# Two attention stages of a two-block network: the first unit's scores later in TensorE's order, no matrix steps behind its turning

## The reference, cut to what matters

```python
def softmax_attend(q, k, v, scale):
    s = jnp.einsum('bqhd,bkhd->bhqk', q, k).astype(jnp.float32) * scale
    p = jax.nn.softmax(s, axis=-1).astype(v.dtype)
    return jnp.einsum('bhqk,bkhv->bqhv', p, v)

def diff_attend(q, k, v, lam, scale):
    s = jnp.einsum('bqhmd,bkhmd->bhmqk', q, k).astype(jnp.float32) * scale
    p = jax.nn.softmax(s, axis=-1)
    a = (p[:, :, 0] - lam * p[:, :, 1]).astype(v.dtype)
    return jnp.einsum('bhqk,bkhv->bqhv', a, v)

y = (jax.nn.sigmoid(g_na) * ((o_na * jax.nn.silu(z_na)) @ w_br_l[0])
     + jax.nn.sigmoid(g_mla) * ((o_mla * jax.nn.silu(z_mla)) @ w_br_l[1])
     + jax.nn.sigmoid(g_diff) * ((o_diff * jax.nn.silu(z_diff)) @ w_br_l[2]))
return y @ w_out_l
```

## Time and profile before

| | us |
|---|---|
| median of 3 runs | 2687.6 |
| lowest and highest | 2682.66, 2688.82 |
| the profiled execution, its own time | 2682.66 |
| its span | 2680.9 |
| TensorE busy in the span | 2482.4 (93%) |
| VectorE busy | 1368.1 (51%) |
| ScalarE busy | 1189.5 (44%) |
| GpSimd busy | 639.4 (24%) |

### The profile page before, as it was taken

How to read it: one execution, slowest core, us unless ns; L and a number is a source line. 1 busy time by engine, 2 the same in 40 slices (tenths; PEclk the granted TensorE clock), 3 DMA queues, 4 the chain that set the end, 5 groups by cost and what they waited for, 6 DMA issues and landing times. The chain is left out here.

```text
span 2680.9 us, 34890 instructions
## 1 busy us (share of the span) xinstructions
PE 2482.4 (93%) x13664; PEld 1960.9 (73%) x13664; DVE 1368.1 (51%) x2120; ACT 1189.5 (44%) x2002; POOL 639.4 (24%) x392
## 2 busy tenths in 40 slices
PE   5997879999998998899997999999999979989988
PEld 3784447888888887568996767577767858768778
DVE  2206667433445766437665534542566444454665
ACT  1824324522327433344654345564366234565362
POOL 1437640000006434110001442003301116403310
PEclk8998988999999999998998999999999999999999
DMA  6326842433324332655664231222222323334333
GB/s 228 86 80 213 290 162 71 118 95 95 102 79 122 107 88 70 219 174 142 190 186 128 63 93 46 59 64 76 71 63 66 92 63 95 107 91 116 89 100 111
DMA packets 416682, 302.11 MB, mean 113 GB/s; under 512 B 10306, under 2 KB 388776, under 8 KB 416520
## 3 DMA queue, kind: packets, MB, share of 16 engines
q1 hardware_dynamic: 415408, 299.45, 38.0%
q10 hardware_dynamic: 1112, 0.44, 0.1%
HBM read 298.80 MB, written 1.05 MB: 112 GB/s over the span
## 5 line engine op out<-in xcount | busy, mean ns | idle before, releaser
L207 POOL TENSOR_TENSOR weights_lo<-wslots,weights_hi 128x1024 fp32r<-128x1024 f32 x158 | 386.4, 2455 | 867.5 <-ACT weights_hi L197 620.5
L197 ACT ACTIVATE weights_hi<-wslots 128x1024 fp32r<-128x1024 f32 x398 | 418.1, 1054 | 288.1 <-PE psum L260 233.0
L260 PE MATMUL psum<-input_hi,weights_hi 128*128 128x512 f32 (+1 forms) x1400 | 501.2, 358 | 4.5 <-PEq L2696 1.8
L260 PE MATMUL psum<-input_hi,weights_lo 128*128 128x512 f32 (+1 forms) x1400 | 488.4, 349 | 0.0
L260 PE MATMUL psum<-input_lo,weights_hi 128*128 128x512 f32 (+1 forms) x1400 | 488.2, 349 | 0.0
L207 DVE TENSOR_TENSOR weights_lo<-wslots,weights_hi 128x1024 fp32r<-128x1024 f32 x240 | 298.7, 1253 | 193.6 <-ACT weights_hi L197 193.3
L260 PEld LDWEIGHTS psum<-input_hi,weights_hi 128*128 128x128 f32 x1400 | 265.1, 189 | 44.4 <-issue 7.5
L260 PEld LDWEIGHTS psum<-input_lo,weights_hi 128*128 128x128 f32 x1400 | 263.8, 188 | 38.3 <-issue 3.4
L260 PEld LDWEIGHTS psum<-input_hi,weights_lo 128*128 128x128 f32 x1400 | 263.9, 189 | 37.7
L260 PE MATMUL psum<-ffn_hidden_hi,weights_hi 128*128 128x512 f32 (+1 forms) x512 | 172.8, 338 | 0.0
L260 PE MATMUL psum<-ffn_hidden_hi,weights_lo 128*128 128x512 f32 (+1 forms) x512 | 172.5, 337 | 0.0
(11 more groups left out here) (439 smaller groups left out, 4857.0 us busy)
## 6 DMA issues: line engine op xcount, KB each, us to landing
wslots<-w_in SPq DMA_DIRECT2D x132, 512.0 KB, 4.0
wslots<-ffn_w SPq DMA_DIRECT2D x128, 512.0 KB, 4.2
wslots<-ada_w SPq DMA_DIRECT2D x96, 512.0 KB, 4.9
wslots<-ssd_w_in SPq DMA_DIRECT2D x49, 512.0 KB, 4.0
wslots<-w_ada SPq DMA_DIRECT2D x48, 512.0 KB, 4.5
wslots<-gla_w_in SPq DMA_DIRECT2D x25, 512.0 KB, 3.8
wslots<-w_br SPq DMA_DIRECT2D x24, 512.0 KB, 3.6
wslots<-ssd_w_out SPq DMA_DIRECT2D x16, 512.0 KB, 4.9
```

The lines of the kernel that those rows point to most:

```text
L197: act.activation(self.part(self.whi_r, n), self.slot(n), ACT.Copy)\
L207: engine.tensor_tensor(self.part(self.wlo_r, n), self.slot(n), self.part(self.whi, n), ALU.subtract)\
L260: ins = pe.matmul(out_of(self.bank(g)), l, r, start=first and i == 0, stop=last and i == len(pairs) - 1, skip_group_check=not (first and l ...
```

## The change

TensorE's order at the start of both functions: `scores(0)` moves behind some of the steps, and all steps up to the first mark now stand ahead of `scores(1)`; none is left behind `turn(0)`. VectorE does `normalise(0)` or `combine(0)` ahead of `vector_second`. In the last unit of `attend_maps`, `middle` lies at a quarter of the unit's steps.

```diff
--- before.py
+++ after.py
@@ -2779,18 +2779,17 @@
                     for _ in range(a, e):
                         next(products)
 
-                lead = marks[0] if near else S // 2
+                lead = 0 if near else S
+                steps(0, lead)
                 scores(0)
-                steps(0, lead)
+                steps(lead, marks[0])
                 for n in range(N):
                     if n + 1 < N:
                         scores(n + 1)
-                    if n == 0:
-                        steps(lead, max(S, lead))
                     turn(n)
                     if n:
                         values(n - 1)
-                    steps(start(n) if n else max(S, lead), marks[n])
+                        steps(start(n), marks[n])
                 values(N - 1)
                 for _ in products:
                     pass
@@ -2867,8 +2866,8 @@
 
                 fill.vector_first(dve)
                 maxima(0)
+                normalise(0)
                 fill.vector_second(dve)
-                normalise(0)
                 for n in range(N):
                     b.split_weights(dve, "dve", fill.lead(start(n)))
                     if n + 1 < N:
@@ -3138,7 +3137,7 @@
         return marks[n - 1] if n else 0
 
     def middle(n):
-        return (start(n) + marks[n]) // 2 if n == N - 1 else marks[n]
+        return (3 * start(n) + marks[n]) // 4 if n == N - 1 else marks[n]
 
     st = ExitStack()
     with st:
@@ -3202,20 +3201,20 @@
                         next(products)
 
                 lead = S // 2
+                steps(0, lead)
                 scores(0)
-                steps(0, lead)
+                steps(lead, marks[0])
                 for n in range(N):
                     gq, h = units[n]
                     if n + 1 < N:
                         scores(n + 1)
-                    if n == 0:
-                        steps(lead, S)
                     turn(n)
                     if n:
                         values(n - 1)
                     if gq and h == 2:
                         turn_rows(gq - 1)
-                    steps(start(n) if n else S, middle(n))
+                    if n:
+                        steps(start(n), middle(n))
                 values(N - 1)
                 for _ in products:
                     pass
@@ -3307,8 +3306,8 @@
 
                 fill.vector_first(dve)
                 maxima(0)
+                combine(0)
                 fill.vector_second(dve)
-                combine(0)
                 for n in range(N):
                     gq, h = units[n]
                     b.split_weights(dve, "dve", fill.lead(start(n)))
```

## The result

The changed kernel is slower: 2710.5 us (median of 4, 2706.4 to 2710.8) against 2685.3 for the kernel before (2682.7 to 2688.8); ratio 1.0102, interval 1.0078 to 1.0128. The ratio takes in all 15 executions of the changed kernel on record (2700.8 to 2720.2, median 2715.0), so it says 27 us where the two medians say 25. The forecast was 2720.2, slower with a chance of 0.94. The profiled execution of the changed kernel took 2715.9 us, 33 more than the profiled one of before.

What follows compares the result with a forecast made beforehand. TensorE's own order of work was taken as the bound. Waits 24.5 us, less 0.3, plus 8.4 for the clock gave 32.6 on 2682.66, so 2715.3; the runs' median lies 4.9 higher, forecast 2720.2, range 2705 to 2734.

Steps and rivals of the forecast that it cites:

- What bounds the kernel: Four stages, pairs with r = 1 and maps in both layers: TensorE's own order of work is the clock.
- Rival C: Late starts absorbed where another engine sets a stage's end; 2700 us if half were absorbed; chance 0.07.
- The stages with r = 0: attend_pairs with r = 0, both layers: the list of steps stays the same, cost 0.
- The waits: New TensorE waits at the four stages' openings: 6.2, 5.8, 6.8 and 5.7, in all 24.5 us.
- the sum: Count of TensorE's waits in each opening, from the stage's issue up to unit 1's steps; 24.5 us over four stages.
- rival B: Clock falls more than once per stage, unit 2 in layer 1's pairs loses 1 us; centre 2730 us, chance 0.15.
- VectorE's swap: Openings: branch split now follows unit 0's normalising, ahead of unit 1's maxima; 2.28 us in layer 0, 1.22 in layer 1.
- The clock: Half-clock work behind the waits in the four stages: 2.1 us each, 8.4 in all, bounds 0 and 22.
- Rival A: Waits without a slower clock, layer 1's being broken by short work: 2711.8 us, chance 0.17.
- Rival E: No change: both effects of Rival D at a smaller size; chance 0.03.
- Rival D: Faster: clock rises sooner at each opening, unit 1's exponentials ready when turn(0) ends; 2680.5 us, chance 0.03.
- The last unit: End of the maps: steps moved by middle are hidden, VectorE's gating product behind subnorm gives -0.3 us in layer 1.

Runs made afterwards that it cites:

- e7: Against the kernel before, the change in attend_pairs alone, attend_maps left as before: ratio 1.0080.
- e6: The changed kernel with identity products put on TensorE in the places where it waits: ratio 1.0115 against the kernel before.
- e4: The changed kernel with the last S/2 steps ahead of the first mark put behind scores(1): ratio 1.0087 against the kernel before.
- e5: The changed kernel with VectorE's maxima of unit 1 ahead of branch and weight splits, layer 0 only: ratio 1.0117 against the kernel before.
- e11: The changed kernel with unit 1's maxima and normalising or combining ahead of VectorE's splits, layer 0 only: ratio 1.0088 against the kernel before.
- e1: The changed kernel again, no edit, in more rounds: 2711.5 us against 2680.7 for the kernel before, ratio 1.0119.
- e2: The changed kernel with VectorE's old order, branch split ahead of unit 0's normalising or combining: ratio 1.0116 against the kernel before.
- e3: The kernel before with only VectorE's swap and the new middle, TensorE's opening as before: ratio 1.0007.

## Why the prediction was right, point by point

*What bounds the kernel.* Right: TensorE's own order and its waits set the length of the four stages, and a wait there is not made up (e7, and every stage's growth against its waits). Rival C falls.

*The stages with r = 0.* Unchanged, as read from the marks: 0.3 and -0.7 us.

*The waits.* Forecast 6.2, 5.8, 6.8, 5.7, in all 24.5. In the rows: 0.22 + 5.46 = 5.7; 4.99, less the 0.45 of before = 4.5; 5.02 + 1.55 + 0.66 = 7.2; 3.21 + 1.20 - 0.30 = 4.1. In all 21.5. Two terms were too large: in the maps I counted 1.1 us at `turn(1)` for combining, and it did not appear. `scores(2)` runs at half clock there (from 1987.33 to the turn at 1990.01, 2.7 us instead of 1.1) and covers the combining, so waits and clock were added as if they did not overlap. But that is the smaller part. At full clock, in e6, the wait is 0.45 us and no more than in the kernel before: the second score product waits for the second exponential (it starts 0.67 us behind the first), so that the pair takes 1.79 us and not 1.1 after such a wait, and the sum had put this at nothing. In the pairs of layer 1 the wait of 0.66 at `scores(3)` was named, but only in rival B.

*Why the waits are there.* The sum had the mechanism right: VectorE at 10.66 us, then unit 1's chain. The sentence ahead of it, that the S steps behind `scores(1)` were the cover that is lost, was only partly right. e4 shows that in layer 0 the two things weighed against each other are TensorE's work between `scores(0)` and `scores(2)` and VectorE's list in the same stretch; e5 and e11 show that VectorE's 4.6 us of splits can be moved along but must be covered somewhere, with 3.95 and 2.7 us of waits instead of 5.5 in the pairs. In layer 1 the sentence holds: half of the steps put back behind `scores(1)` shortened the wait ahead of step 16 from 5.02 to 0.71 and from 3.21 to 1.16 us (e4).

*VectorE's swap.* I said only that the branch split had lain in the wait for the exponentials, and priced it inside the sum. Its own share of TensorE's waiting is 4.8 us under the new order (e1 against e2) and 2.4 under the old one with the new middle (e3). The stages differ by more, 7 to 9 us and 5.7, but the rest is clock and noise of single profiles.

*The clock.* Forecast 8.4 us, 2.1 behind each wait. Measured in the rows: 3.3, 2.0, 2.0 and 4.2, in all 11.5, of which e6 shows 6 to 8 as what the stages' lengths gain without it. So the sum was closer than its terms: the waits were 3.0 too high and the clock 3.1 too low, the two errors cancel, and that the total of 32.6 meets the 32 of the profiles is luck in that part. The Trainium skill ("TensorE: Matmul & The Clock Gate", What's actually happening) has an idle array gated down; the trace agrees at each of the four waits, and e6 shows that work without use keeps the clock up. Rival A, waits alone, falls as a mechanism, though its 2711.8 us is nearer to the first measured median than the forecast. By the profiles that is chance: the stages are 32 and 34 us longer. Rival B falls: no stage has a second slow stretch behind its waits, and 11.5 is less than its 16 to 22. Rival E falls with the interval. Rival D falls: nothing was ready when `turn(0)` ended.

*The last unit.* `finish` starts 1.29 us behind the start of `values(7)` instead of 1.64, -0.35 forecast as -0.3; the products at the end are hidden. Timeline after:

```profile
2633.54 1.16 PE L3184 MATMUL psum<-att_v,probT 128*128 128x128 f32 x8 [1.35 <-ACT probT L3238]
...
2634.83 0.68 DVE L3287 COPY diff_rows<-psum 128x512 f32<-128x512 f32 x1
...
2638.29 0.66 PE L3194 MATMUL psum<-ident,diff_rows 128*128 128x128 f32 x4 [1.82 <-DVE diff_rows L3298]
```

The final turning waits 1.82 us, not 2.89: two more steps, some 0.7 us, stand in front of it, and the rows are ready 0.35 sooner. It runs at full clock (0.66 us, not 1.12). `values(7)` in turn waits 1.35 us instead of 0.68, since those steps are gone from ahead of it. The waits are the same in e3 (1.36 and 1.82), under the old opening, so they are the middle's doing. It was not run by itself, so what it is worth in time stays open.

*What stays open.* The effect of the clock on the time itself (7 us) is below what e6's runs can show. The opening stretch at half clock differs between executions of the same code and puts up to some 2 us of noise on a stage's length; the maps of layer 0 show it, +4.8 in one profile of the changed kernel and +7.2 in the other with the same wait of 4.99.

## What to carry to other kernels

Before moving an instruction of the engine that sets the pace, write down what the helper engines have queued between the two results that it will wait for, and compare that with the work left in between; a chain that is hidden everywhere else in a loop can be bare in its first iteration. Filler steps are worth most where a chain is open, and least at the very start. And look at what stands in a helper's queue ahead of the next link of a chain: a transfer or split that is itself waiting there (1.60 us here) holds up work that was ready, and moving it behind that link made this kernel 0.2 to 0.3% faster than it was before the change.

## What the runs showed of the hardware

The wait of 5.46 us on TensorE cost more than itself: the next 6.6 us of work ran at a granted 0.50, 3.3 us lost. The waits need not be that long: in the maps of e3, layer 0, a slower stretch came behind 1.45 and 0.45 us, while in the pairs of e11 the transposes behind a wait of 1.55 us took 1.04, full speed. Where a wait was cut by short work, as in the maps of layer 1 (3.21, then 1.20 us), the slow stretch went on across both. 25 products of the identity in the wait kept the clock at 1.00; each took 0.225 us (1754.84 to 1760.47 in e6).

How long the slow stretch at a stage's start lasts differs with unchanged code. Windows from the start of `attend_maps` in layer 0, changed kernel, its first profiled execution:

```profile
1971.50:1974.30 2.80, 2.67 (x6) 2.15 (x7) 0.00 (x0) 1.87 (x1) 0.00 (x0) 0.50 0.62 143
1974.30:1980.00 5.70, 5.70 (x24) 3.83 (x23) 2.21 (x7) 2.28 (x5) 0.00 (x0) 0.99 0.35 117
```

and in e1:

```profile
1955.50:1961.50 6.00, 5.85 (x13) 3.31 (x13) 0.00 (x0) 1.88 (x1) 0.00 (x0) 0.50 0.62 175
```

2.8 us at 0.50 in the one, 6.0 in the other.
